# Quadrant sums of the down weights, built in DRAM by transfers that GpSimd begins, in a two-layer encoder kernel

## The reference

```python
def squared_relu_mlp(u, w_up, w_down):
    return jnp.square(jax.nn.relu(u @ w_up)) @ w_down

for i in range(DEPTH):
    ...
    h = h + rmsnorm(mixed, norm_mix_post[i])
    f = squared_relu_mlp(rmsnorm(h, norm_mlp_pre[i]), w_up[i], w_down[i])
    h = h + rmsnorm(f, norm_mlp_post[i])
```

## Time and profile before

| | |
|---|---|
| median of 2 runs | 1336.41 us (1336.33 to 1336.49) |
| span of the profiled execution | 1335.1 us |
| TensorE busy | 1324.6 us, 99% |
| VectorE, ScalarE, GpSimd busy | 687.9, 588.6, 114.5 us |
| moved by DMA | 137.75 MB, mean 103 GB/s |

### The profile page before, as it was taken

One profiled execution on the slowest core, in us unless ns is written; L12 is line 12 of the kernel. 1 busy time (PEld: TensorE's weight loads), 2 busy tenths in 40 slices (PEclk: granted clock), 3 DMA queues, 4 the chain that ended last, 5 costly groups with the idle time before them and its releaser, 6 DMA issues.

```text
span 1335.1 us, 18387 instructions
## 1 busy us (share of the span) xinstructions
PE 1324.6 (99%) x6935; PEld 1093.5 (82%) x6935; DVE 687.9 (52%) x1080; ACT 588.6 (44%) x1105; POOL 114.5 (9%) x131
## 2 busy tenths in 40 slices
PE   9999999999999999999999999999999999999998
PEld 7778888888788888888888898777898888888886
DVE  5586677887436443223443364875474432244333
ACT  6645455676435443213332344765354322133321
POOL 0044352660000000000000000000000000000000
PEclk9999999999999999999999999999999999999999
DMA  7343433243432323233222233112223323322221
GB/s 221 104 126 100 130 103 102 93 163 112 159 109 80 99 93 108 95 127 95 94 98 92 79 100 119 48 64 80 79 81 102 114 98 110 95 94 95 97 100 72
DMA packets 75551, 137.75 MB, mean 103 GB/s; under 512 B 6342, under 2 KB 16854, under 8 KB 75478
## 3 DMA queue, kind: packets, MB, share of 16 engines
q1 hardware_dynamic: 71184, 134.76, 31.2%
q10 hardware_dynamic: 4294, 2.00, 0.8%
HBM read 133.41 MB, written 2.93 MB: 102 GB/s over the span
## 4 chain that ended last, share of the span: by engine, by line
PE 97%; DVE 1%; DMA 1%; ACT 1%; issue 1%; DVEq 0%; ACTq 0%
PE G L1733 64%; PE X L1733 12%; PE X L1756 7%; PE G L1806 3%; PE X L1806 3%; PE X L1912 1%; PE X L1921 1%; PE X L1995 1%; PE X L2210 1%; PE X L2182 1%; PE X L2200 1%; DMA raw<-in_w_mem_kv 1%; PE X L1934 1%; PE X L1974 1%; PE X L1983 0%
## 5 line engine op out<-in xcount | busy, mean ns | idle before, releaser
L1118 DVE TENSOR_TENSOR wlo<-raw,whi 128x1024 fp32r<-128x1024 f32 x207 | 252.6, 1226 | 441.9 <-ACT whi L567 440.8
L567 ACT ACTIVATE whi<-raw 128x1024 fp32r<-128x1024 f32 x207 | 217.7, 1058 | 421.3 <-PE G L1733 209.7
L1733 PE MATMUL G<-uhi,whi 128*128 128x512 f32 x736 | 294.3, 400 | 0.2 <-DVE ulo L1135 0.2
L1733 PE MATMUL G<-uhi,wlo 128*128 128x512 f32 x736 | 287.1, 390 | 0.0
L1733 PE MATMUL G<-ulo,whi 128*128 128x512 f32 x736 | 286.7, 390 | 0.0
L1733 PEld LDWEIGHTS G<-uhi,whi 128*128 128x128 f32 x736 | 138.2, 188 | 31.2 <-issue 1.1
L1733 PEld LDWEIGHTS G<-uhi,wlo 128*128 128x128 f32 x736 | 138.1, 188 | 29.5 <-DVE wlo L1166 0.2
L1733 PEld LDWEIGHTS G<-ulo,whi 128*128 128x128 f32 x736 | 138.3, 188 | 28.4
L1733 PE MATMUL G<-whi,hidhi 128*128 128x512 f32 x256 | 99.6, 389 | 0.0
L1733 PE MATMUL G<-whi,hidlo 128*128 128x512 f32 x256 | 99.6, 389 | 0.0
L1733 PE MATMUL G<-wlo,hidhi 128*128 128x512 f32 x256 | 99.6, 389 | 0.0
(11 more groups left out here) (342 smaller groups left out, 2240.5 us busy)
## 6 DMA issues: line engine op xcount, KB each, us to landing
raw<-in_w_up SPq DMA_DIRECT2D x64, 512.0 KB, 3.8
raw<-in_w_down SPq DMA_DIRECT2D x64, 512.0 KB, 3.5
raw<-in_ssd_w_in SPq DMA_DIRECT2D x20, 512.0 KB, 3.6
raw<-in_w_mem_kv SPq DMA_DIRECT2D x16, 512.0 KB, 3.6
raw<-in_ssd_w_out SPq DMA_DIRECT2D x16, 512.0 KB, 3.5
raw<-in_swa_w_in SPq DMA_DIRECT2D x16, 512.0 KB, 3.8
raw<-in_ssd_w_in SPq DMA_DIRECT2D x16, 384.0 KB, 3.4
csrow<-cs_rows SPq DMA_DIRECT2D x16, 384.0 KB, 4.4
```

Of the source, the lines that this page charges most:

```text
L567: act.activation(whi[q][:, :, :], raw[q % 2][:, :, :], ACT.Copy).then_inc(hi_done, 1)
L1118: dve.tensor_tensor(wlo[q][:, :, :], raw[q % 2][:, :, :], whi[q][:, :, :].bitcast(F32), ALU.subtract).then_inc(lo_done, 1)
L1733: mm = pe.matmul(o, st, mv, start=(kt == 0 and fresh and not go_on), stop=(q == total - 1 and k == 1), skip_group_check=True)
```

## The change

For each layer a DRAM scratch `tsum` of four blocks, 2048 x 512 each, is added. With the down weight as quadrants B11, B12, B21, B22, the blocks become T1 = B11 + B21, T2 = B11 + B12, T3 = T1 + B12 and T4 = T3 + B22. Each block is made in four row groups r of 512 rows; a step x (0 to 7) is a plain copy (x = 0, 1, 4, 6) or an adding transfer (x = 2, 3, 5, 7), from DRAM to DRAM. Transfer n has x = n // 4 and r = n % 4, so each of the four chains goes one step further every four transfers, and a transfer waits for the one four before it. GpSimd begins all of them: two ahead of each unit for layer 0, and for layer 1 one in every two panels from panel 68 on, at the end of its program. The sums are not read by anything.

```diff
--- before.py
+++ after.py
@@ -352,6 +352,9 @@
             else:
                 eng.wait_ge(panel_done, p_end)
 
+        tsum = [nc.dram_tensor(f"tsum{i}", (4, FF // 2, 512), F32, kind="Internal").ap() for i in range(2)]
+        sum_in = [sem(f"sum_in{r}") for r in range(4)]
+
         block = ctx.enter_context(nc.Block())
 
 
@@ -508,12 +511,31 @@
                                  bcast[:, 2, gh].unsqueeze(2).to_broadcast([P, SR, P]),
                                  ALU.mult).then_inc(s_di, 1)
 
+            def weight_sum(i, n):
+
+                x, r = divmod(n, 4)
+                rows = slice(512 * r, 512 * r + 512)
+                w = a["w_down"][i]
+                b11, b12 = w[0:2048, 0:512][rows, :], w[0:2048, 512:1024][rows, :]
+                b21, b22 = w[2048:4096, 0:512][rows, :], w[2048:4096, 512:1024][rows, :]
+                t1, t2, t3, t4 = (tsum[i][j][rows, :] for j in range(4))
+                if 8 * i + x > 0:
+                    ps.wait_ge(sum_in[r], 16 * (8 * i + x))
+                if x in (0, 1, 4, 6):
+                    dst, src = {0: (t1, b11), 1: (t2, b11), 4: (t3, t1), 6: (t4, t3)}[x]
+                    ps.dma_start(dst, src).then_inc(sum_in[r], 16)
+                else:
+                    dst, src = {2: (t1, b21), 3: (t2, b12), 5: (t3, b12), 7: (t4, b22)}[x]
+                    ps.dma_start(dst, src, accum_op=ALU.add).then_inc(sum_in[r], 16)
+
             ps.wait_ge(consts, 4)
             ps.wait_ge(bc_in, 48)
             ps.wait_ge(aftdt_done, 1)
             for v in range(UNITS):
                 g, c = divmod(v, NT)
                 gh = slice(SR * g, SR * g + SR)
+                for n in range(2 * v, 2 * v + 2):
+                    weight_sum(0, n)
                 if v == 0:
                     skip_diagonal(0)
                 ps.wait_ge(cs_in[v % 3], 16 * (v // 3) + 16)
@@ -542,6 +564,11 @@
                                      tot[:, c, gh].unsqueeze(2).to_broadcast([P, SR, HD]),
                                      ALU.mult).then_inc(s_decayed, 1)
 
+            for n in range(32):
+                ps.wait_ge(panel_done, 4 * B_F0 + 2 * n)
+                weight_sum(1, n)
+            for r in range(4):
+                ps.wait_ge(sum_in[r], 16 * 16)
 
         @block.scalar
         def _(act):
```

## The result

The changed kernel takes 1373.39 us (median of two runs, 1370.92 and 1375.86) against 1336.41: 1.0277 times the time before, interval 1.0233 to 1.032, slower by 37 us. The profiled execution spans 1369.2 us, 34.1 more than before.

A forecast was written before the change was run, and what follows sets the result against it. The prediction took TensorE's work plus stalls to bound the kernel: 1335.1 us profiled, plus 42 us from GpSimd's new waits and nothing from the other items, gives 1377, with 1.3 us around it 1378 us; range 1340 to 1444.

The forecast's parts named there:

- What bounds the kernel: Whole kernel: the time is TensorE's work, busy 1324.6 of 1335.1 us, plus any stall put into it.
- Item 1, issues: GpSimd begins two transfers before each unit's csrow pass, 1 us each; they fit in the late units' slack: 0.
- Item 2, length: DMA engines' time per 1.05 MB transfer: middle taken, 4.64 us a copy and 7.88 us an add.
- the low ends: Transfer lengths if reading and writing overlap: 3.24 us a copy, 6.48 an add; about 6 us late in all.
- Item 3, new waits: Layer 0's state-space stage: GpSimd waits for the transfer four earlier, holding up units 11 to 15: 42 us.
- The queue drains in time: Rival: copies at load rate, adds at twice that; not slower, 0 to 8 us, 1342 us; chance 0.30.
- Item 4, starved loads: Weight loads beside the transfers: landing 5.3 us at halved shares, under the memory panels' limit of 6.1: nothing.
- GpSimd's issues or starved loads: Rival without a full queue: 4 us issues give +16, or 8 us landings in memory panels +15: 1352; chance 0.13.
- they fit: Layer 1's 32 transfers behind panel 68: 200 us of work in 338 us with 0.70 of the engines free.
- signs of being right: Units 12 to 14: csrow passes after tsum waits, TensorE idle some 40 us, DMA share 0.9 or more, rest unchanged.
- wrong on size: Sign in the trace: a tsum copy's packet time far from 4.64 us.
- wrong on mechanism: Signs: long GpSimd spans at DMA lines, raw loads landing after over 6 us with ScalarE waiting, or TensorE idle beyond 410.

The follow-up runs named there:

- the small transfers: The changed kernel with every issue and wait kept, but each transfer moving 16 rows instead of 512: 1342.6 us, 1.0045 times the kernel before.
- the quiet place: The changed kernel with all 64 transfers moved into the feed-forward stages, evenly spaced, none in the scan: 1344.35 us, 1.0055 times the kernel before.
- ScalarE's new order alone: The kernel before, no transfers, with ScalarE doing each unit's xtok copy and exponential ahead of its split of a later panel: 1348.5 us, 1.0085.

## Why the prediction came near for the wrong reason

The time, 1373.4 against 1378, and the side were right; the mechanism that gave 42 us did not happen. That the number agreed was luck: 42 us for a wait that never bound stood where the runs show 37 of late loads and issues, for which the sum had nothing.

- *What bounds the kernel*: right. Every loss is idle or slowed TensorE.
- *Item 1, issues.* The size was near: a pair costs 1.3 us, where 2 were taken. "Two issues at 1 us fit in all" was wrong: the small transfers show 5.9 us. The 5.4 us of slack for unit 12 was read off GpSimd's own waits; but TensorE already waited 1.67 us for that unit, which the item passed over. In the whole change the 6 us need not add to the rest: begun behind the passes, the transfers gained nothing.
- *Item 2, length.* **The first step that failed**, a size. The taken middle was 4.64 and 7.88 us; the traces give 3.18 and 6.23, near or under the low ends 3.24 and 6.48. Both rates were in the trace of before; the middle was chosen for want of a row with both sides in HBM, and a load, whose two sides overlap, was the nearer row.
- *Item 3, new waits.* Its working with the measured prices: (16 x 3.18 + 12 x 6.23)/0.598 = 210 us, done at 61.8 + 210 + 1.5 = 273, and unit 15 may start until 303.8. The queue drains, no wait binds, 0 us. Copies with and without waits agree within 1 us. The rival *The queue drains in time* had this part right, and took from it that nothing would be left, 1342, which was wrong.
- *Item 4, starved loads.* **The second step that failed**, a term put at nothing. Halved shares gave 5.3 us; loads land after 8.1 at the median where it counts. Its own working then gives ((8.1 + 2.3)/2 - 4.2) x 16 = 16 us, and 17 were lost in those panels. This was the rival *GpSimd's issues or starved loads*, at 0.13 and +15: the right mechanism, priced for one place. The item let a load share the engines half and half; beside the load at 193.34 us GpSimd's packets had three times the engines' time of SP's. It also costs 6.5 us before them, where panels of 5.45 us should bear 8.6 us of landing: in the first three windows the medians are 4.8, 9.5 and 4.9 us, with single loads up to 15. The limit was set against an even landing.
- *Layer 1*: "they fit" was true, and they cost 7 to 10 us even so, most of it where short panels begin.
- *TensorE's clock* was in no item; the rows price it at about 12 us. It follows the stalls and not the traffic: with copies the lowest window of the five is 0.93, with the quiet place 1.00, and in the kernel before with ScalarE's new order alone, which has stalls and no transfer, 0.93 again.
- *What would show it*: of the signs of being right only the DMA share came, 0.94 and 0.89. The "wrong on size" and "wrong on mechanism" signs both came, loads over 6 us with ScalarE behind them (its wait for memory loads rose from 3.3 to 20.6 us, for `w_up` from 32.2 to 54.9) and idle TensorE beyond 410 us.

Shown: without the bytes 6 of the 37 us are left, so the bytes cost some 31; no wait for another transfer binds in the trace, and with copies such waits cost nothing; another engine and queue lose at least as much; the same transfers in another stage and spacing cost 8. Argued from rows only: the share of the clock, and that the loads wait for the engines and not for the memory. Open: how each stall divides between the late load, the two `raw` buffers and the order of tasks on ScalarE and VectorE (a third `raw` buffer was not tried), and whether the stage or the spacing of the transfers counts more.

## What to carry to other kernels

Background traffic is priced by the landing time that it gives the loads around it, against what the buffers can bear in the shortest panels there, and not by whether the DMA engines have a free share: here loads doubled in time, and the same 67 MB cost 37 us in pairs within the scan and 8 one by one in the feed-forward stages. Where a load waits for the buffer of the panel two back, a late load can be paid again two panels on, and a short stall of TensorE can be paid once more in its clock. An engine that works in order hands a late load on to everything behind its split. When a forecast's time comes true, look for its own wait in the trace before believing it.

## What was not expected of the hardware

- An adding transfer from DRAM to DRAM takes 6.23 us of the 16 engines per 1.05 MB where a copy takes 3.18; alone, 5.1 and 3.4 us of elapsed time for each further one. The profile's bytes leave the second read out.
- The issue row on GpSimd is 0.63 us for a copy of 512 rows, 1.06 for an add of them, and 0.53 for a copy of 16 rows of 64 KB; a pair delays what stands behind it by 1.3 us.
- Beside eight adds, 512 KB loads one after the other land after 8.1 to 8.5 us instead of 3.4 to 3.8; beside copies, after 8.7 to 11.2. Two transfers of 1.05 MB begun together held a load for up to 15.2 us in the change.
- The four stalls of 2.9 to 4.9 us came with stretches at half clock on a TensorE that was otherwise at the full one (0.50 from 290 to 295 us). In the kernel with the order alone, stalls of 1.9 to 2.7 us did so too (0.69 from 255 to 260 us, behind 2.28); the one of 1.67 us in the kernel before did not (1.00).
